# Gates stored where merged blocks go, three ring slots for early expert weights, and edits to the chain and the first turn of a decoder block

## Chip, core and metric

The kernel runs on one core of a Trainium2 chip. The time is device microseconds for one launch, the median of several runs. Four compute engines (TensorE, VectorE, ScalarE, GpSimd) each run their own instruction stream and meet at semaphores; SyncE (SP) issues the transfers.

## What is computed

One decoder layer on 256 tokens of width 1024, all in float32:

```python
h = rms_norm(x, g_mix);  proj = h @ w_in + b_in          # 1024 x 6656
q, k, v, cb, cc, cx, ga, gc = split(proj)
y_attn = sliding_window_attention(rope(q), rope(k), v, sinks) @ w_attn_o
y_conv = (cb * causal_short_conv(cc * cx, w_conv)) @ w_conv_o
merged = sigmoid(ga) * y_attn + sigmoid(gc) * y_conv
x = x + merged @ w_out
h = rms_norm(x, g_ffn)
x = x + moe_ffn(h, ...)   # router takes 4 of 32 experts; per expert
                          # a = g*sigmoid(1.702 g)*(u+1), then a @ w_down
return rms_norm(x, g_final)
```

The 32 experts' weights (up, gate, down, 1024 x 1024 each) are 403 MB, nearly all that the kernel reads.

## The kernel before, in words

**First stage.** The weights of the projections come as 38 pieces of 1 MB (NP1), n = 0 to 37: 26 of w_in (NIN), then w_conv_o and w_attn_o in turn (8), then w_out (4). They land in three small slots in turn. For each piece ScalarE makes a rounded copy wH (L754), and GpSimd (L1319, first half m = 0) and VectorE (L966, m = 1) the remainder wL. TensorE multiplies in three terms: low x wH, high x wH, high x wL (project_T L402, project L415), where high and low are the two parts of the activations. A loop of four turns (L477) does q, conv_C, conv_x, conv_B and the two gates with the attention of a group of heads between them. Then the branch projections (L527) are gated and merged by VectorE (L1091 to L1097), split into mH and mL, and the output projection (L560) adds to x1. In it TensorE also turns x1 (turn_x1) and multiplies it with the router (route).

**Ring.** Eight slots of 2 MB hold expert weights; an expert has six pieces (two of up, gate, down each), and load_expert (L352) issues them on SP's queue in order. In the first stage the same memory holds other things: an "area" is half a slot. Areas 0 to 2 are the three slots for pieces, hH/hL lie in 3, 4, zH/zL in 5, 6, aH/aL in 7, 8, the gates ga and gc in 9, 10, the keys kz in 11, wH and wL in 12 to 15. The first turn of loads waits accordingly (L366 to L373): for areas under 12 for the last branch block and merged_ready, for the rest for the last projection. PHYS gives the order in which slots are used. mH lies in tile mt, mL in tile normed.

**Between the stages.** VectorE scales x1 (scale_x1 L1100), ScalarE and GpSimd cut it into three bfloat16 parts for gathering (cut_high, rest_of, cut_mid, low_of), the inverse root mean square comes by GpSimd (L1304), then VectorE picks the top 4 (L1140 to L1164), TensorE ranks the tokens per expert (L574 to L578), VectorE makes the one-hot G, and TensorE gathers the tokens of expert 0.

**Experts.** For each expert (expert, L656) TensorE runs wide into bank 4 (up), gathers for the next expert, wide into bank 5 (gate), scatters the previous expert's result into banks 0 to 3, turns the activation, and runs wide into bank 7 (down). The first expert does turn_wgt and spread_down_bias instead of a scatter: x1 and the weighted down bias are put into banks 0 to 3 (L651, L653). weights_used frees ring slots. Four experts are straight code, then a loop of seven turns of four. The bias rows that wide adds come to their place by twelve small transfers on SP's queue (L349), on which ScalarE waits before it splits piece 36.

## Time and profile before

| | |
|---|---|
| median of 3 runs | 1216.02 us (1215.77 to 1217.55) |
| profiled execution | 1215.88 us, its span 1214.0 us |
| TensorE busy | 1123.0 us (93%) |
| VectorE, ScalarE, GpSimd busy | 364.9, 236.6, 129.7 us |
| read from HBM | 446.06 MB, 368 GB/s over the span |
| chain that ended last | TensorE 49%, DMA 41%, VectorE 4%, ScalarE 2% |

```profile
GB/s 295 140 166 145 165 154 180 178 391 408 344 429 428 426 427 429 428 427 430 427 429 429 427 430 426 429 430 426 430 426 429 431 426 430 426 429 431 426 429 201
```

This row of the page has the transfers' rate in 40 equal slices of 30 us: eight slices of first stage, then expert weights, with a lower slice at 300 to 330 us. "Idle before" behind a row is the engine's idle time ahead of it and what ended it. The granted clock is TensorE's, as a share of 2.4 GHz.

### The profile page before, as it was taken

The numbers are of one execution on the slowest core, as the hardware profiler recorded it, in microseconds if no ns is written. First come the engines' busy times: TensorE is split into PE (matmuls) and PEld (weight loads), VectorE is DVE, ScalarE is ACT, GpSimd is POOL, SyncE is SP. The second block draws the span as 40 slices with busy tenths as digits, with TensorE's granted clock in tenths as the row PEclk, the third lists the DMA queues.
The fourth block names the chain that finished last, engine by engine and source line by source line (L and its number), as shares of the span: only waits on it lengthen the run. The fifth ranks groups of instructions, "written<-read, shape, count | busy, mean of one in ns | idle before, by whom it ended". The sixth has DMA issues, their size and how long they took to land.

```text
span 1214.0 us, 18031 instructions
## 1 busy us (share of the span) xinstructions
PE 1123.0 (93%) x7446; PEld 574.7 (47%) x7446; DVE 364.9 (30%) x687; ACT 236.6 (19%) x410; POOL 129.7 (11%) x98
## 2 busy tenths in 40 slices
PE   8999999888999999999999999999999998999996
PEld 6899999883333333433333333333333333333332
DVE  5867785663121111111211211111111111111112
ACT  5566654351000100100010001000100110011001
POOL 4453444430000000000000000000000000000000
PEclk9999999998999999999999999999999999999999
DMA  9444445599899999999999999999999999999994
GB/s 295 140 166 145 165 154 180 178 391 408 344 429 428 426 427 429 428 427 430 427 429 429 427 430 426 429 430 426 430 426 429 431 426 430 426 429 431 426 429 201
DMA packets 71250, 447.93 MB, mean 369 GB/s; under 512 B 5433, under 2 KB 45717, under 8 KB 46645
## 3 DMA queue, kind: packets, MB, share of 16 engines
q1 hardware_dynamic: 70752, 446.75, 89.1%
q10 hardware_dynamic: 469, 0.77, 0.2%
q8 instruction: 21, 0.34, 0.1%
q14 instruction: 8, 0.07, 0.0%
HBM read 446.06 MB, written 1.05 MB: 368 GB/s over the span
## 4 chain that ended last, share of the span: by engine, by line
PE 49%; DMA 41%; DVE 4%; ACT 2%; issue 2%; POOL 1%; SPq 0%; POOLq 0%; DVEq 0%; ACTq 0%
PE psum L610 27%; DMA ring<-in_w_gate 20%; DMA ring<-in_w_up 20%; PE psum L411 14%; PE psum L423 2%; PE psum L586 2%; POOL wL L1319 1%; PE psum L634 1%; DVE work L1202 1%; DVE work L1207 1%; DVE work L1204 1%; ACT work L898 1%; DMA ring<-in_w_in 1%; PE psum L601 1%; PE psum L594 1%
## 5 line engine op out<-in xcount | busy, mean ns | idle before, releaser
L610 PE MATMUL psum<-ring,work 128*64 128x512 f32 x3072 | 688.4, 596 | 48.7 <-DMA ring<-in_w_up 25.5
L610 PEld LDWEIGHTS psum<-ring,work 128*64 128x64 f32 x3072 | 211.8, 137 | 473.6 <-issue 369.9
L1200 DVE TENSOR_SCALAR work<-psum 128x512 f32<-128x512 f32 x32 | 22.1, 692 | 422.5 <-PE psum L610 422.5
L1319 POOL TENSOR_TENSOR wL<-ring,wH 128x1024 fp32r<-128x1024 f32 x38 | 103.0, 2720 | 111.5 <-ACT wH L754 111.5
L411 PE MATMUL psum<-hL,wH 128*128 128x256 f32 x384 | 110.5, 288 | 3.5 <-POOL wL L1319 2.9
L411 PE MATMUL psum<-hH,wH 128*128 128x256 f32 x384 | 109.2, 284 | 0.0
L411 PE MATMUL psum<-hH,wL 128*128 128x256 f32 x384 | 109.1, 284 | 0.0
L1202 DVE TENSOR_SCALAR work<-psum 128x512 f32<-128x512 f32 x32 | 22.1, 692 | 284.5 <-PE psum L610 284.5
L1357 POOL COPY chosen<-pick 96x64 bf16 (+1 forms) x32 | 7.5, 234 | 886.9 <-PE psum L634 886.9
L966 DVE TENSOR_TENSOR wL<-ring,wH 128x1024 fp32r<-128x1024 f32 x38 | 77.2, 2034 | 38.5 <-ACT wH L754 38.5
L754 ACT CAST wH<-ring 128x1024 fp32r<-128x1024 f32 x76 | 76.3, 1048 | 29.0 <-PE psum L411 18.1
L411 PEld LDWEIGHTS psum<-hL,wH 128*128 128x128 f32 x384 | 74.2, 193 | 6.4 <-issue 3.3
L411 PEld LDWEIGHTS psum<-hH,wH 128*128 128x128 f32 x384 | 74.3, 194 | 0.0
L411 PEld LDWEIGHTS psum<-hH,wL 128*128 128x128 f32 x384 | 74.2, 193 | 0.0
L907 ACT ACTIVATE work<-work 128x512 f32<-128x512 f32 x32 | 20.2, 630 | 249.6 <-DVE work L1202 249.6
L864 ACT COPY work<-psum 128x64 f32<-128x64 f32 x33 | 7.0, 213 | 301.7 <-PE psum L594 301.7
L621 PE MATMUL psum<-work 64*128 64x512 f32 x256 | 63.6, 615 | 0.7 <-ACT work L903 0.7
L903 ACT COPY work<-psum 128x512 f32<-128x512 f32 x32 | 18.8, 587 | 230.5 <-PE psum L610 230.5
L586 PEld LDWEIGHTS psum<-G,h2b 128*128 128x128 bf16 x1584 | 49.2, 99 | 27.1 <-issue 27.1
L586 PE MATMUL psum<-G,h2b 128*128 128x64 bf16 x1584 | 53.1, 195 | 1.1 <-DVE G L1171 1.1
L621 PEld LDWEIGHTS psum<-work 64*128 64x128 f32 x256 | 22.0, 186 | 41.8 <-issue 40.2
L634 PEld LDWEIGHTS psum<-cst,work 128*128 128x128 f32 x128 | 17.8, 209 | 40.4 <-DVE work L1207 39.7
(199 smaller groups left out, 917.2 us busy)
## 6 DMA issues: line engine op xcount, KB each, us to landing
ring<-in_w_up SPq DMA_DIRECT2D x64, 2048.0 KB, 32.7
ring<-in_w_gate SPq DMA_DIRECT2D x64, 2048.0 KB, 35.4
ring<-in_w_down SPq DMA_DIRECT2D x64, 2048.0 KB, 34.6
ring<-in_w_in SPq DMA_DIRECT2D x26, 1024.0 KB, 4.9
ring<-in_w_conv_o SPq DMA_DIRECT2D x4, 1024.0 KB, 5.2
ring<-in_w_attn_o SPq DMA_DIRECT2D x4, 1024.0 KB, 5.2
ring<-in_w_out SPq DMA_DIRECT2D x4, 1024.0 KB, 5.6
xres<-in_x SPq DMA_DIRECT2D x2, 512.0 KB, 4.2
```

The costliest lines, as they stand in the source:

```text
L411: mm = pe.matmul(bank(b, m * T, T), w[:, par, m, k, :], x[:, k, :], start=(k == 0 and x is low), stop=(k == KB - 1 and w is wL))
L423: mm = pe.matmul(bank(b[t], t * PW, PW).rearrange("p (m n) -> p m n", m=2), x[:, k, t * P:(t + 1) * P], w[:, par, :, k, :], start=(k == 0 ...
L586: mm = pe.matmul(bank(6, k * CW, CW), h2b[:, part, t, k * P:(k + 1) * P], G[:, t, :], start=(t == 0 and part == 0), stop=(t == TT - 1 and ...
L610: mm = pe.matmul(psum[64 * h:64 * h + 64, b, :], src[:, k, :], w[:, k2, h * 512:(h + 1) * 512], start=(bias_of is None and k == 0), stop=( ...
L621: pe.matmul(bank(2 * t + h), S[64 * h:64 * h + 64, t * P:(t + 1) * P], ysb[64 * h:64 * h + 64, :], start=False, stop=False, skip_group_che ...
L634: tr = pe.transpose(bank(5, b * P, P), act_runs[:, b // RUN, :, b % RUN], ident)
L754: nc.scalar.copy(wH[:, par, m, :, :], slot(s).rearrange("p (k n) -> p k n", k=KB)[:, :, m * P:(m + 1) * P],).then_inc(wH_ready, 1)
L907: nc.scalar.activation(sg, gm, ACT.Sigmoid, scale=ALPHA).then_inc(sig_ready, 1)
L966: v.tensor_tensor(wL[:, p2, 1, :, :], slot(s).rearrange("p (k n) -> p k n", k=KB)[:, :, P:2 * P], wH[:, p2, 1, :, :].bitcast(F32), ALU.sub ...
L1200: v.tensor_scalar(uc, psum[:, 4, :], LIMIT, -LIMIT, ALU.min, ALU.max)
L1202: v.tensor_scalar(gm, psum[:, 5, :], LIMIT, None, ALU.min).then_inc(gmin_ready, 1)
L1319: g.tensor_tensor(wL[:, par, 0, :, :], slot(s).rearrange("p (k n) -> p k n", k=KB)[:, :, 0:P], wH[:, par, 0, :, :].bitcast(F32), ALU.subtr ...
```

## The change

Gates go to mt and normed, where merged blocks are written afterwards; hH to aL move up one area, the keys down to area 3. Ring slots 5, 2 and 3 come first, with pieces 0 and 1 issued among the loads of the first stage, and the waits of the first turn are by area. The projections take the terms with wH first and wait for wL behind them. One wait on merged_ready goes. Between the stages: five matmuls before the ranks, the spread inside the first gather, turn_wgt ahead of the first expert, two VectorE steps less, the last scale_x1 behind the mean square. spread_down_bias moves to expert 29, and the last group of four experts is straight code too.

```diff
@@ line 54
-PHYS = [2, 3, 4, 5, 1, 0, 6, 7]
+PHYS = [5, 2, 3, 4, 1, 0, 6, 7]
+EARLY = 2
...
@@ line 82
     c[:, C_M1:C_M1 + 2 * P] = np.where((dist >= 0) & (dist < P), 0.0, MASKED)
-    c[:, C_IOTA:C_IOTA + CW] = np.where(np.arange(CW) < CAP, np.arange(CW), -5 * T)
+    c[:, C_IOTA:C_IOTA + CW] = np.where(np.arange(CW) < CAP, np.arange(CW) - NEVER, -5 * T - NEVER)
...
@@ line 135
         mt_at = -(-nc.sbuf_base // 32) * 32
-        sb("mt", [P, KB, T])
+        mt = sb("mt", [P, KB, T])
...
@@ line 168
             return ring_at + s * KB * PW * 4
-        hH, hL = parts("hH", at_slot(3), [P, KB, T]), parts("hL", at_slot(4), [P, KB, T])
-        zH, zL = parts("zH", at_slot(5), [P, KB, T]), parts("zL", at_slot(6), [P, KB, T])
-        aH, aL = parts("aH", at_slot(7), [P, KB, T]), parts("aL", at_slot(8), [P, KB, T])
+        hH, hL = parts("hH", at_slot(4), [P, KB, T]), parts("hL", at_slot(5), [P, KB, T])
+        zH, zL = parts("zH", at_slot(6), [P, KB, T]), parts("zL", at_slot(7), [P, KB, T])
+        aH, aL = parts("aH", at_slot(8), [P, KB, T]), parts("aL", at_slot(9), [P, KB, T])
...
         mH, mL = parts("mH", mt_at, [P, KB, T]), parts("mL", normed_at, [P, KB, T])
-        ga = slot(9).rearrange("p (k t) -> p k t", k=KB)
-        gc = slot(10).rearrange("p (k t) -> p k t", k=KB)
-        kz = slot(11).rearrange("p (g h t) -> p g h t", g=NKV, h=2)
+        ga = mt
+        gc = normed.rearrange("p t (k c) -> p (t k) c", c=T)
+        kz = slot(3).rearrange("p (g h t) -> p g h t", g=NKV, h=2)
...
@@ line 319
+            def load_run(e, c, r):
+                s = phys((c * EP + r) % RING)
+                src = experts[r // RUNS][bass.ds(e, 1), :, r % RUNS, :, :]
+                sp.dma_start(ring[:, s, :], src.rearrange("a p r n -> p (a r n)")).then_inc(slot_full[s], 16)
+            load_run(0, 0, 0)
...
@@ line 342
                 n += 1
+                if n == NIN + 5:
+                    sp.wait_ge(blocks_done, 2 * NIN)
+                    load_run(0, 0, 1)
...
@@ line 351
                 for r in range(EP):
-                    s = phys((c * EP + r) % RING)
-                    wait(r, s)
-                    src = experts[r // RUNS][bass.ds(e, 1), :, r % RUNS, :, :]
-                    sp.dma_start(ring[:, s, :], src.rearrange("a p r n -> p (a r n)")).then_inc(slot_full[s], 16)
+                    if wait(r, phys((c * EP + r) % RING)):
+                        load_run(e, c, r)
...
                         p = c * EP + r
+                        if first and p < EARLY:
+                            return False
...
                                     slot_split(max(n for n in range(NP1) if n % RING1 == area) + RING1)
-                                elif area < 12:
+                                elif area < 8:
+                                    sp.wait_ge(blocks_done, 2 * (NIN + 2 * NKV - 1))
+                                elif area < 10:
                                     sp.wait_ge(blocks_done, 2 * (NIN + 2 * NKV))
-                                    sp.wait_ge(merged_ready, NKV)
...
                                     sp.wait_ge(blocks_done, 2 * NP1)
+                        return True
...
@@ line 385
                     e = sp.value_load(eid[0:1, bass.ds(j, 1)], min_val=0, max_val=NE - 1)
-                    load_expert(e, 0, lambda r, s: None)
+                    load_expert(e, 0, lambda r, s: True)
...
@@ line 405
                         between()
+                    pe.wait_ge(wH_ready, n * 2 + (m + 1))
+                    for k in range(KB):
+                        for x in (low, high):
+                            pe.matmul(bank(b, m * T, T), wH[:, par, m, k, :], x[:, k, :], start=(k == 0 and x is low),
+                                      stop=False)
...
                     for k in range(KB):
-                        for w, x in ((wH, low), (wH, high), (wL, high)):
-                            mm = pe.matmul(bank(b, m * T, T), w[:, par, m, k, :], x[:, k, :],
-                                           start=(k == 0 and x is low), stop=(k == KB - 1 and w is wL))
+                        mm = pe.matmul(bank(b, m * T, T), wL[:, par, m, k, :], high[:, k, :], start=False, stop=(k == KB - 1))
...
                 high, low = src
-                pe.wait_ge(wL0_ready, n + 1)
-                pe.wait_ge(wL1_ready, n + 1)
+                pe.wait_ge(wH_ready, n * 2 + 2)
                 def block(t, ks):
-                    for k in ks:
-                        for x, w in ((low, wH), (high, wH), (high, wL)):
+                    for k, x, w in [(k, x, wH) for k in ks for x in (low, high)] + [(k, high, wL) for k in ks]:
+                        if True:
+                            if w is wL and k == ks[0] and t == 0:
+                                pe.wait_ge(wL0_ready, n + 1)
+                                pe.wait_ge(wL1_ready, n + 1)
...
@@ line 555
-            pe.wait_ge(merged_ready, NKV)
...
@@ line 569
+            for n in range(WARM):
+                pe.matmul(bank(2), ident, cst[:, 0:512], start=True, stop=True)
...
@@ line 577
-            def gather(nth):
+            def gather(nth, between=None):
...
                 for k in range(KB):
+                    if k == KB // 2 and between is not None:
+                        between()
...
@@ line 612
-            def scatter(nth, chunk):
+            def scatter(nth, chunk, fresh=False):
...
                         pe.matmul(bank(2 * t + h), S[64 * h:64 * h + 64, t * P:(t + 1) * P],
-                                  ysb[64 * h:64 * h + 64, :], start=False, stop=False, skip_group_check=True,
+                                  ysb[64 * h:64 * h + 64, :], start=fresh, stop=False, skip_group_check=True,
...
@@ line 639
                 for t in range(TT):
-                    tr = pe.transpose(bank(6, t * P, P)[0:NE], wgt[:, t, 0:NE], ident)
+                    tr = pe.transpose(bank(3, t * P, P)[0:NE], wgt[:, t, 0:NE], ident)
...
@@ line 648
                     for h in range(2):
-                        pe.matmul(bank(2 * t + h), ident, xres[:, t, h * 512:(h + 1) * 512], start=True, stop=False,
+                        pe.matmul(bank(2 * t + h), ident, xres[:, t, h * 512:(h + 1) * 512], start=False, stop=False,
...
+            def at(j, n):
+                return isinstance(j, int) and j == n
...
                 pe.wait_ge(picked, j + 1)
-                if j is not first_expert:
+                if not at(j, 0):
                     pe.wait_ge(S_ready, j)
-                if j is first_expert:
-                    turn_wgt()
                 wide(4, xe, c, 0, uses, 0)
-                if j is first_expert:
+                if at(j, 0):
...
                 wide(5, xe, c, RUNS, uses, 1)
-                if j is first_expert:
+                if not at(j, 0):
+                    scatter(j, j, fresh=at(j, 1))
+                if at(j, NE - UNROLL + 1):
                     spread_down_bias()
-                else:
-                    scatter(j, j)
...
             pe.wait_ge(low_ready, NKV)
-            gather(0)
-            spread_r(0, 5)
+            gather(0, lambda: spread_r(0, 5))
+            turn_wgt()
             pe.wait_ge(bias_out, 16 * 12)
-            first_expert = 0
-            for c in range(UNROLL):
-                expert(c, c, lambda p: 16 * (p // RING + 1))
-            first_expert = None
-            with pe.Fori(1, NE // UNROLL) as it:
+            def group(it):
...
                     expert(it * UNROLL + c, c, uses)
+            group(0)
+            with pe.Fori(1, NE // UNROLL - 1) as it:
+                group(it)
+            group(NE // UNROLL - 1)
...
@@ line 908
             act_e.wait_ge(wT_turned, 1)
-            nc.scalar.copy(wT[:, :], psum[0:NE, 6, 0:256]).then_inc(wT_ready, 1)
+            nc.scalar.copy(wT[:, :], psum[0:NE, 3, 0:256]).then_inc(wT_ready, 1)
...
@@ line 971
             v.memset(u[:, :, 0:2], 0.0)
-            v.memset(pos[:, :, NE:NE + 1], NEVER)
+            v.memset(pos[:, :, NE:NE + 1], 0.0)
...
@@ line 1097
+            sums = small[:, 12:20].rearrange("p (t i) -> p t i", t=TT)
...
@@ line 1124
                 n += 1
-                scale_x1(i)
+                if i < NKV - 1:
+                    scale_x1(i)
...
                     rest_of(i)
+                if i == NKV - 2:
+                    dve.wait_ge(ssq_ready, 2 + 2 * (NKV - 1))
+                    steps.link(v.tensor_reduce(small[:, 6:8], sums[:, :, 0:NKV - 1], AX.X, ALU.add))
+                    steps.link(v.tensor_scalar(small[:, 6:8], small[:, 6:8], 1.0 / D, EPS, ALU.mult, ALU.add))
...
             dve.wait_ge(ssq_ready, 2 + 2 * NKV)
-            steps.link(v.tensor_reduce(small[:, 6:8], small[:, 12:20].rearrange("p (t i) -> p t i", t=TT), AX.X, ALU.add))
-            ms(6)
+            v.scalar_tensor_tensor(small[:, 8:10], sums[:, :, NKV - 1:NKV].rearrange("p t i -> p (t i)"), 1.0 / D, small[:, 6:8],
+                                   ALU.mult, ALU.add).then_inc(ms_ready, 1)
+            scale_x1(NKV - 1)
...
@@ line 1149
             steps.link(ins)
-            steps.link(v.tensor_copy(topf, topi[:, :, :]))
...
                 ins = v.tensor_tensor(onehot[:, t], count_up[:, 0:NE].unsqueeze(1).broadcast_to([P, TOPK, NE]),
-                                      topf[:, t, 0:TOPK].unsqueeze(2).broadcast_to([P, TOPK, NE]), ALU.is_equal)
+                                      topi[:, t, 0:TOPK].unsqueeze(2).broadcast_to([P, TOPK, NE]), ALU.is_equal)
...
@@ line 1161
                                               -NEVER, Mf[:, :, :], ALU.add, ALU.mult))
-            steps.link(v.tensor_scalar(pos[:, :, 0:NE], pos[:, :, 0:NE], NEVER, None, ALU.add))
...
@@ line 1212
+                dve.wait_ge(gathered, nth + 1)
...
                     dve.wait_ge(weights_used, used)
...
```

## Rows read from the trace of the kernel before

**Rows 1.** Chain that ended last, in order of time: start us, us, what

```profile
298.62 1.06 PE psum L651 x2
...
306.00 1.05 PE psum L653 x2
...
315.71 6.87 PE psum L610 x32
...
342.87 6.87 PE psum L610 x32
...
620.89 3.68 PE psum L610 x16
...
709.00 3.68 PE psum L610 x16
...
1153.25 35.41 DMA ring<-in_w_gate
```

**Rows 2.** Windows: us, five engines' busy time, TensorE's clock, DMA share, GB/s

```profile
306.00:314.00 8.00, 7.54 (x34) 2.87 (x36) 2.31 (x8) 0.59 (x1) 0.23 (x1) 1.00 0.34 115
360.00:1180.00 820.00, 759.92 (x4714) 286.72 (x4714) 149.02 (x375) 75.91 (x129) 6.79 (x29) 1.00 1.01 428
```

**Rows 3.** SP's queue in order of time: start us, us, line, what

```profile
235.05 8.85 SPq L349 DMA_DIRECT2D bias<-bcut  x12
...
267.06 0.80 SPq L357 DMA_DIRECT2D ring<-in_w_up  x2
286.05 3.76 SPq L357 DMA_DIRECT2D ring<-in_w_gate  x2
...
312.10 0.33 SPq L357 DMA_DIRECT2D ring<-in_w_up  x1
```

**Rows 4.** First turn, in order of time on SP, ScalarE, VectorE and TensorE

```profile
16.93 0.40 SPq L307 DMA_DIRECT2D ring<-in_w_in  x1
...
31.27 1.99 ACT L754 CAST wH<-ring 128x1024 fp32r<-128x1024 f32 x2
...
35.85 3.78 DVE L953 COPY work<-work 32x512 f32<-32x512 f32 x4
...
34.79 10.17 PE psum L411 x72
```

**Rows 5.** Branch and output projections: waits, timeline, one window, bias transfers' landings

```profile
PE psum L411 <- POOL wL L1319: 1.1, 3, 0.4
...
239.15 0.58 PE L423 MATMUL psum<-wH,mL 128*128 128x256 f32 x1 [2.88 <-DVE mL L1096]
...
240.00:242.00 2.00, 2.00 (x11) 2.00 (x11) 1.64 (x1) 0.26 (x1) 1.78 (x1) 0.50 0.19 45
...
246.76 2.00 ACT L754 CAST wH<-ring 128x1024 fp32r<-128x1024 f32 x2 [6.50 <-PE psum L423]
...
L349 SPq DMA_DIRECT2D bias<-bcut x12: 605/606/1530, 235.0 to 243.3; - x12
...
DMA to landing us min/median/max: 1.9/2.9/5.1
```

**Rows 6.** From x1 to the first expert: timeline and a window; opening matmuls last

```profile
267.02 0.76 DVE L1124 TENSOR_TENSOR xres<-psum,xres 128x256 f32<-128x256 f32 x2 [3.68 <-PE psum L423]
...
271.24 0.41 DVE L1141 SCALAR_TENSOR_TENSOR work<-psum,small,brt 128x32 f32<-128x32 f32 x2 [0.92 <-PE psum L553]
...
275.67 2.72 PE L586 MATMUL psum<-G,h2b 128*128 128x64 bf16 x48 [1.09 <-DVE G L1171]
...
281.31 8.13 PE L610 MATMUL psum<-ring,work 128*64 128x512 f32 x32
...
289.37 1.57 PE L586 MATMUL psum<-G,h2b 128*128 128x64 bf16 x48
...
274.00:283.00 9.00, 6.58 (x65) 4.51 (x67) 5.95 (x27) 1.86 (x3) 0.00 (x0) 0.50 1.03 404
...
2.62 6.73 PE L466 MATMUL psum<-ring 128*128 128x512 f32 x10 [2.62 <-POOL ring L1309]
```

## The prediction

> **What bounds the kernel now.** I read the chain of waits first, then the load queue, then the windows of the stretch between the two stages. From 620.9 us on the chain alternates between weight landings and short stretches of TensorE. Three experts take 88.11 us (620.89 to 709.00), 29.37 each, or 4.895 per 2 MB piece; TensorE alone needs 27.15 for an expert, seen where its weights are there early (315.71 to 342.87) [rows 1]. So each expert of the late part has 2.22 us of slack on TensorE, and the load stream sets the end. In the bulk the stream moves 428 GB/s and the DMA engines are full. Only between 306 and 314 us do they stand at a 0.34 share, so 5.3 us are empty [rows 2]. The queue's issues say why: piece 8 goes out at 286.05, when the first expert's first slot is free, but piece 12 only at 312.10 [rows 3]. The ring of eight was full, and TensorE was busy with the down bias, 8 pairs from 298.62 to 307.05 [rows 1]. From piece 12's issue to the landing of piece 189, the last on which the chain waits (1153.25 + 35.41, so 1188.67 [rows 1]), it is 876.6 us for 178 pieces; 25.3 us follow to the end of the span. Thus three things can shorten the kernel: an earlier first slot release (now 286.05), no hole after it, and less behind the last landing.
>
> **Slots for expert weights.** Piece 0 goes out behind the small loads, before the fourth w_in piece; piece 1 behind the fifth branch piece. With the gates in mt and normed, three slots are no longer tied to merged_ready. In the loop over the first stage the DMA engines are about half idle, so I cost the transfers at nothing. The cover: the fourth w_in piece is issued at 16.93 and not split by ScalarE before 31.27 [rows 4]; 4.9 us of queue ahead of it leave more than 4 us. If that cover were gone, piece 0 would cost up to 4.9 us. What do early slots bring? The third one brings little: its load still stands in SP's program behind the last branch loads and the twelve bias moves, which hold SP for 8.85 us from 235.05 [rows 3]. With two pieces there, six remain. Four start at about 240.5 (the end of the bias moves, 243.9, less 3.5 us won before it, below) and are in by 260.2; pieces 6 and 7 wait for wH and wL, free after the last projection (267.06 now, some 260.5 after), and are in by about 270.5. Without the early pieces the fill would end at about 280. I get the first release at 277.8 below. So the early slots are worth 1 to 2 us; the ring is full again, and the release decides.
>
> The Trainium skill ("DMA: Bandwidth & Descriptors", Queues, rings and completion order) says that an issuing engine's transfers are consumed in ring order on each DMA engine. That speaks against loading early: pieces 3 to 5 stand behind piece 0. By that rule alone the first stage could lose the 4.9 us; the rows on ScalarE's first use give it room. This rule is the third rival.
>
> **Bias spread from the first expert to the 30th.** The eight pairs take 8.43 us wherever they stand [rows 1]. In the first expert they made the hole. Without them TensorE frees slots 0, 3.4 (16 matmuls of wide, half of the 6.87 [rows 1]), 9.1, 12.6, 20.1 and 23.5 us after the first release, against 4.895 us a piece: 0.5 us of hole stays. From piece 8's issue to piece 189's landing I expect 876.6 + 4 x 4.895 + 0.5 = 896.7 us. With the present 286.05 that is 1182.7 instead of 1188.67: 6.0 us gained. But at expert 29 (counted from 0) the 8.43 us lie on TensorE ahead of wide(7), and only two experts with 2.22 us of slack each follow. 8.43 - 4.44 = 4.0 us come back at the end. The ring covers the loads meanwhile (8.4 us is under two pieces of eight). Bounds: 0 if the last landing still decides, 8.4 if nothing is absorbed. The unrolled last group I cost at nothing: the present first group is straight code as well and its cadence is the loop's; bounds 0 to 1 us. No less, because it does no less work.
>
> **High half first, and the dropped wait.** In the branch projections TensorE waits three times for wL, 1.1 us in all [rows 5]; wH is there 2.4 us before wL, so the 16 matmuls with wH cover it: -1.1. In the first turn TensorE waits 2.9 us for wL before block 3, until 34.79 [rows 4], and runs some 3 us of it at half clock. With the high half it can start at 32.3. Behind that comes q's rotation on VectorE, whose copies start at 35.85 [rows 4] and which ends near 41.7, so scores cannot follow block 4 much earlier, and then the softmax chain. I take -2.4, bounds 0 and -3.6.
>
> The first output projection no longer waits for all merged blocks. It starts at 239.15, 2.88 us after its predecessor, and its first matmuls run at the lower clock, 0.50 in 240 to 242 [rows 5]. The fourth merged block is needed only after 36 matmuls, 4.3 us: covered. That frees 2.9 us of waiting and 1.7 of slow clock, 4.6. But ScalarE stands behind it: it splits piece 36 only at 246.76 and, by its program, not before all bias moves have landed. The last is issued at 243.3 and they take 1.9 to 5.1 us [rows 5], so it is there at 245.2 or later. With 3.5 us from before it is 241.7. Then follow the split (1.9), two square sums (1.2), cut_high (.6) and turn_piece (.6): route(0) can start at 246.1, where it starts at 252.67 now, though TensorE would be there at 244.6. So of 4.6 us only 3.1 arrive. Sum for the end of the last projection: 2.4 + 1.1 + 3.1 = 6.6 us earlier (bounds 1 and 9).
>
> **The chain from x1 to the first expert.** Now 286.05 - 267.02 = 19.0 us lie between x1 and the first release. All of it runs at half clock from 270 on [rows 6]. VectorE: scale_x1(3) now follows the rstd input and ScalarE's cut, rest_of(3) ends at +4.85 instead of +3.3, and the logits, now at +4.22, start 0.65 later. Dropping the copy to topf gives back 0.21, dropping the addition of NEVER 0.23. TensorE: 5 warming matmuls, ten instructions, start at +3.9. In the opening the same ten took 6.73 us, five at 0.86 and five at 0.43 [rows 6]. I take the clock to rise after the third: they end at +9.35, later than M_ready at +7.6. So M's matmuls come 2.1 us later than now, and the gather starts at +10.55 instead of +8.65: 1.9 us lost. In return it runs at full clock: 48 matmuls and the spread take 2.05 (1.57 and 0.64 at 289.37, less overlap) against 3.64 now (275.67 to 279.3); ScalarE's copy of slot_r is hidden by the interleaving (0.27); turn_wgt leaves the path (0.68); the first 16 of wide take 3.44 against 4.53 (of the 8.13 that all 32 take [rows 6]). 1.9 - 1.6 - 0.3 - 0.7 - 1.1 = -1.7. Bounds: -4.5 (clock never low), +4.4 (low for all ten and through the expert's start).
>
> The Trainium skill ("TensorE: Matmul & The Clock Gate", What's actually happening) says that the slow clock is the default and activity releases it. By that the warming pays; the rows agree that the clock was 0.50 while TensorE waited and ran small matmuls. No row here shows what ten large ones do at this place.
>
> **Sum**, against the profiled 1214.0 us of span and 1215.88 of time (the median of the runs is 1216.02, the same within 0.01%): first release 286.05 - 6.6 - 1.7 = 277.75; + 896.7 = 1174.45; + 25.3 = 1199.8; + 4.0 = 1203.8; + 1.9 outside the span = 1205.7.
>
> **Rivals.** (1) Forecast as above, 0.50, its own range 1202 to 1209. (2) More arrives: the bias moves land in time, block 3 gains 3.6 and the warming ends before M_ready: 1.5 + 1.2 + 2.3 less, 1200.7; 0.14. For it: every lost us above is a place where two engines finish within 2 us. (3) The first stage gains nothing, because weights ahead of w_in pieces eat it, or VectorE's chain gives it back: + 6.6, 1212.3; 0.13. Against it: ScalarE waits for a landing only once. (4) The warming runs slow throughout and ends at +12.5: + 6.1, 1211.8; 0.15. (5) The change doesn't act as it says, the slots being filled anyway: only the title's part falls, 1 to 2 us, 1207.2; it lies within (1). (6) Slower: the stream itself. Landings now go to slots in another order. The 896.7 us hang on 428 GB/s; each per cent is 9.0 us, and from 1.4% (below 422) the kernel is slower than before; at 2% it is 1223.6. Against it: the DRAM reads are the same. 0.04; with mixtures of (3), (4) and a bias spread not absorbed (+4.4) it makes 0.06 slower in all.
>
> **Numbers.** 0.2% is 2.4 us, about what can be told from no change. Faster 0.88, within 0.2% 0.06 ((3) and (4) together, or either with an unabsorbed spread), slower 0.06. The range takes in (2) to (4): 1199 to 1213; some 2 in 10 lie outside.
>
> **What would show it.** The first ring release near 278; no empty stretch of DMA at 300 to 310 but one ahead of the first release, some 6 us; the last landing on which the chain waits near 1174; the last wide starting about 4 us after its weights are in; matmuls at 239 without a wait; a wait at route(0); the M matmuls 2 us later against x1. It is wrong if the stream doesn't follow the first release, or if the bias spread costs its full 8.4 us late.

## The result, and the profile of the changed kernel

The changed kernel takes 1206.97 us (median of 5 runs, 1206.07 to 1210.74) where the kernel before, run beside it, takes 1216.3 (1215.77 to 1217.92): a ratio of 0.9925, 95% interval 0.9909 to 0.9942. The prediction was 1205.7 within 1199 to 1213. The profiled run took 1206.97, with a span of 1205.2.

Below, columns and views are those of the section of rows; "release" is the issue of piece 8, the first load that waits for a slot used by the first expert. SP's queue of the changed kernel:

```profile
188.92 0.37 SPq L308 DMA_DIRECT2D ring<-in_w_attn_o  x1
...
235.00 8.51 SPq L360 DMA_DIRECT2D bias<-bcut  x12
243.61 1.01 SPq L326 DMA_DIRECT2D ring<-in_w_gate  x2
...
263.15 0.80 SPq L326 DMA_DIRECT2D ring<-in_w_up  x2
278.94 3.76 SPq L326 DMA_DIRECT2D ring<-in_w_gate  x2
...
300.71 3.76 SPq L326 DMA_DIRECT2D ring<-in_w_up  x2
```

The last output projection ends (263.15, pieces 6 and 7 go out) 3.9 us earlier than before, the release is 7.1 us earlier, and piece 12, which stood behind the bias spread, 11.4 us earlier [rows 3]. But the bias moves still begin at 235.00, as before: up to there the changed first stage has won nothing. The load of attn_o at 188.92, issued behind the loop over the heads, is even 1.3 us later (187.63 before).

The timeline of ScalarE and TensorE from the output projections to the first expert's end. L571 is route, the product of one of the four parts of x1 with the router (route(0) the first, route(3) the last); Mb is M, the table of chosen experts, from which TensorE makes the ranks:

```profile
244.82 2.00 ACT L777 CAST wH<-ring 128x1024 fp32r<-128x1024 f32 x2 [5.04 <-DMA bias<-bcut]
...
248.66 1.08 PE L571 MATMUL psum<-wr,work 128*128 128x32 f32 x8 [0.95 <-ACT work L895]
...
265.44 1.08 PE L571 MATMUL psum<-wr,work 128*128 128x32 f32 x8 [0.79 <-DVE work L1163]
266.35 4.54 PE L590 MATMUL psum<-cst 128*128 128x512 f32 x10
271.05 0.19 PE L593 MATMUL psum<-Mb,tri 128*128 128x32 bf16 x1 [0.16 <-DVE Mb L1190]
...
272.20 0.86 PE L607 MATMUL psum<-G,h2b 128*128 128x64 bf16 x24 [0.86 <-DVE G L1200]
...
293.90 0.75 PE L655 MATMUL psum<-cst,work 128*128 128x128 f32 x4 [2.37 <-DVE work L1236]
```

ScalarE waits 5.04 us for the bias moves, and through it TensorE at route(0). The five warming matmuls of the code are ten instructions in the trace, called the ten warming matmuls below. They take 0.45 us each, so the clock never fell here, and they end 0.16 us before M is ready. In the first expert there is a new wait of 2.37 us: TensorE is ready to turn the activation before VectorE has made it, since the bias spread no longer stands between. Windows of the stretches after it:

```profile
276.00:280.00 4.00, 4.00 (x21) 1.51 (x18) 1.38 (x6) 0.34 (x1) 0.00 (x0) 1.00 0.40 137
...
296.00:298.00 2.00, 2.00 (x6) 0.49 (x4) 1.21 (x6) 0.00 (x0) 0.00 (x0) 0.50 1.03 442
300.00:304.00 4.00, 4.00 (x22) 1.33 (x20) 0.00 (x0) 0.00 (x0) 0.00 (x0) 1.00 0.67 213
...
360.00:1180.00 820.00, 764.08 (x4756) 289.10 (x4754) 146.22 (x365) 74.61 (x127) 6.55 (x28) 1.00 1.01 428
```

The DMA engines stand empty for 4 x 0.60 = 2.4 us ahead of the release and 4 x 0.33 = 1.3 us around the issue of piece 12, where 5.3 us were empty before [rows 2]. Behind the new wait TensorE ran at 1.2 GHz (0.50 granted) from 296.0 to 299.4. In the bulk the stream moves 428 GB/s, as before. The end of the chain of waits:

```profile
1082.84 35.85 DMA ring<-in_w_gate
...
1124.31 1.05 PE psum L672 x2
...
1131.68 1.05 PE psum L674 x2
...
1188.41 7.11 PE psum L631 x32
```

The last landing on which the chain waits is 1118.69, at expert 29. Then come the eight bias pairs (1124.31 to 1132.73), and from there to the last wide the chain is compute alone: the weights are always there first. Before, it still waited for the landing at 1188.67 [rows 1]. One part of the difference between the two spans is not the change: from the issue of the output's store to the end of the span it is 5.4 us in the profile before (1208.58 to 1214.0) and 4.4 us here (1200.83 to 1205.2), and 4.3 to 4.4 in all other profiles but one.

### The profile page after: what moved, and what is told of

Its sections match the earlier page's. It is cut to its first block, busy times and chain, and to the rows that moved or that the text cites. A ratio compares the mean times of both kernels' runs of the same rounds, so it can differ in the third digit from the quotient of the medians.

```text
span 1205.2 us, 18121 instructions
## 1 busy us (share of the span) xinstructions
PE 1122.0 (93%) x7456; PEld 573.6 (48%) x7456; DVE 367.8 (31%) x686; ACT 236.5 (20%) x410; POOL 130.1 (11%) x98
## 4 chain that ended last, share of the span: by engine, by line
PE 50%; DMA 38%; DVE 6%; ACT 2%; issue 2%; SPq 1%; DVEq 0%; ACTq 0%
PE psum L631 30%; DMA ring<-in_w_gate 20%; DMA ring<-in_w_up 17%; PE psum L424 8%; PE psum L428 4%; PE psum L607 2%; PE psum L655 1%; DVE work L1231 1%; DVE work L1236 1%; DVE work L1233 1%; PE psum L441 1%; ACT work L921 1%; DVE wL L989 1%; ACT wH L777 1%; DMA ring<-in_w_in 1%
## 5 line engine op out<-in xcount | busy, mean ns | idle before, releaser
L424 PE MATMUL psum<-hL,wH 128*128 128x256 f32 x384 | 95.3, 286 | 1.7 <-ACT wH L777 1.1
L424 PE MATMUL psum<-hH,wH 128*128 128x256 f32 x384 | 94.1, 283 | 0.0
L989 DVE TENSOR_TENSOR wL<-ring,wH 128x1024 fp32r<-128x1024 f32 x38 | 80.8, 2131 | 40.4 <-ACT wH L777 40.4
L428 PE MATMUL psum<-hH,wL 128*128 128x256 f32 x384 | 53.9, 283 | 0.3 <-POOL wL L1349 0.3
L428 PEld LDWEIGHTS psum<-hH,wL 128*128 128x128 f32 x384 | 49.5, 192 | 0.5 <-POOL wL L1349 0.5
L655 PE MATMUL psum<-cst,work 128*128 128x128 f32 x128 | 23.9, 309 | 16.0 <-DVE work L1236 16.0
## 6 DMA issues: line engine op xcount, KB each, us to landing
ring<-in_w_up SPq DMA_DIRECT2D x64, 2048.0 KB, 32.7
```

The source lines that it names most:

```text
L424: pe.matmul(bank(b, m * T, T), wH[:, par, m, k, :], x[:, k, :], start=(k == 0 and x is low), stop=False)
L428: mm = pe.matmul(bank(b, m * T, T), wL[:, par, m, k, :], high[:, k, :], start=False, stop=(k == KB - 1))
L655: tr = pe.transpose(bank(5, b * P, P), act_runs[:, b // RUN, :, b % RUN], ident)
L989: v.tensor_tensor(wL[:, p2, 1, :, :], slot(s).rearrange("p (k n) -> p k n", k=KB)[:, :, P:2 * P], wH[:, p2, 1, :, :].bitcast(F32), ALU.sub ...
```

## Experiments

The kernel before was timed again beside each group; its medians were 1216.7 (beside no_warming, old_order, no_early_slots, merged_wait), 1216.5 (bias_first, only_bias_moved, bias_at_28, bias_at_24) and 1216.0 (the last four of the table). The intervals of the ratios are about ±0.0015, 2 us, and so a single difference of one or two microseconds between two medians is not settled by them. The changed kernel was not timed beside the others; against it, a difference of medians and one of ratios can come apart: no_early_slots is 3.5 us longer by medians and 1.7 by ratios, merged_wait 3.3 and 2.3, no_collision 2.9 and 1.8 shorter. Of the kernels made from the changed one, only quarter_first and all_three have an interval that doesn't overlap with its own. What carries the other verdicts are the stations of the profiled run: the attn_o load (end of the loop over heads), the issue of pieces 6 and 7 (end of the last projection), the release, piece 12, and the span. Each kernel has one profile, and it need not be a typical run: no_collision's is the shortest of its five, those of only_bias_moved, no_early_slots and quarter_first are the longest of theirs.

| kernel | median us | ratio to before | attn_o | last proj. | release | piece 12 | span |
|---|---|---|---|---|---|---|---|
| before | 1216.3 | | 187.63 | 267.06 | 286.05 | 312.10 | 1214.0 |
| changed | 1206.97 | 0.9925 | 188.92 | 263.15 | 278.94 | 300.71 | 1205.2 |
| no_warming | 1208.99 | 0.9931 | 189.09 | 263.49 | 280.74 | 302.09 | 1207.6 |
| bias_first | 1207.77 | 0.9930 | 189.04 | 263.27 | 279.04 | 305.10 | 1206.2 |
| old_order | 1208.38 | 0.9930 | 188.74 | 264.81 | 280.59 | 302.09 | 1206.6 |
| no_early_slots | 1210.49 | 0.9939 | 188.85 | 263.90 | 279.65 | 301.43 | 1210.2 |
| merged_wait | 1210.24 | 0.9944 | 188.13 | 264.32 | 281.45 | 303.22 | 1209.3 |
| only_bias_moved | 1214.71 | 0.9978 | 188.63 | 266.63 | 287.17 | 308.76 | 1214.5 |
| bias_at_28 | 1204.76 | 0.9905 | 189.02 | 263.42 | 279.20 | 300.95 | 1203.3 |
| bias_at_24 | 1205.83 | 0.9917 | 186.20 | 260.56 | 276.33 | 297.77 | 1202.1 |
| no_collision | 1204.04 | 0.9910 | 186.17 | 260.61 | 276.38 | 296.45 | 1200.8 |
| bias_wait_later | 1206.44 | 0.9922 | 188.03 | 261.04 | 278.17 | 299.94 | 1204.6 |
| quarter_first | 1202.72 | 0.9890 | 189.05 | 263.97 | 279.74 | 299.82 | 1203.1 |
| all_three | 1199.63 | 0.9867 | 185.63 | 258.65 | 275.79 | 295.87 | 1196.8 |

**Without the warming matmuls.** The loop of WARM matmuls behind route(3) is left out:

```
-            for n in range(WARM):
-                pe.matmul(bank(2), ident, cst[:, 0:512], start=True, stop=True)
```

> The kernel after without the five warming matmuls ahead of the ranks. Theory (activity there keeps the clock up): the clock is 0.5 from some 270 us to the first expert as before the change, the gather's 48 matmuls take 2.7 instead of 1.6 us, the first slot release comes some 2.9 us later (near 282 instead of 278.9) and the time is 2 to 3 us above the kernel after (1209 to 1210). Rival (the clock was up there by chance, the warming itself only delays): release and time the same or up to 0.5 us less.

TensorE now waits for M, and its clock is low from 268.9 to 275.7:

```profile
271.36 0.21 PE L591 MATMUL psum<-Mb,tri 128*128 128x32 bf16 x1 [4.51 <-DVE Mb L1188]
```

From last projection to release it is 17.25 us for 15.79. The warming is worth 1.5 us here, about half of the 2.9 expected, and it delays nothing. The time agrees in its direction (2.0 us by medians, 0.7 by ratios) and settles nothing by itself.

**Bias spread back in the first expert.** All else is as changed:

```
-                if not at(j, 0):
-                    scatter(j, j, fresh=at(j, 1))
-                if at(j, NE - UNROLL + 1):
-                    spread_down_bias()
+                if at(j, 0):
+                    spread_down_bias()
+                else:
+                    scatter(j, j)
```

(Its first matmul of each pair also starts the bank afresh again, as before the change.)

> The kernel after with the down bias spread in the first expert again, all else as after. Theory: TensorE now waits 2.4 us for VectorE in the first expert and falls to the lower clock there; the 8.4 us fill that wait, so piece 12 is released some 4.5 us later than after (305.2 for 300.7) and the DMA is empty for as long; at the end 3.5 us of lag go. Sum about 1 us above the kernel after (1208). Rival (the prediction's sum holds): 2.0 us above. Rival (the late bias costs its whole 8.4 us): 4 us below.

Piece 12 goes out 4.4 us later, the wait of 2.37 us and the fall of the clock are gone, and the chain ends on landings again. The span is 1.0 us longer. So in this pair of profiles the move to expert 29 by itself, with all else in place, gains 1 us: 4.4 at the start, 3.5 given back at the end. The medians, 0.8 us apart, agree and don't settle it.

**The old order of the projections.** project_T and project take wH and wL of each k together, and wait for both first:

```
-                    pe.wait_ge(wH_ready, n * 2 + (m + 1))
-                    for k in range(KB):
-                        for x in (low, high):
...
                     pe.wait_ge((wL0_ready, wL1_ready)[m], n + 1)
                     for k in range(KB):
...
+                        for w, x in ((wH, low), (wH, high), (wL, high)):
...
```

> The kernel after with the terms of each projection in the old order and the wait for wL ahead of them. Theory (with the high half first the first turn collides VectorE with GpSimd: scores come later, although TensorE is earlier; in the branch projections it saves the waits): the second turn of the loop begins 1 to 1.5 us earlier than after, the branch projections get back 1.1 to 1.3 us of waits, the time stays within 1 us of after (1206 to 1208). Rival (the early weights made the first turn late, the order helps everywhere): the first turn stays late or gets later, and the time is 1.3 to 4 us above after.

The loop over heads ends at the same time as in the changed kernel, within 0.2 us. The new order gains 1.3 us in the branch stage (bias moves at 236.16 for 235.00) and 0.5 in the projections, but in the first turn nothing. That part of the theory fell, and with 1208.38 so did its time (1206 to 1208). Yet the collision it spoke of is gone in this run: VectorE's add of the first turn took 0.69 us, 2.77 in the changed kernel. What hid it is that block 3 starts at 35.84 for 32.90, and that the opening came 0.5 us later. What VectorE has in it, no_collision tests.

**No early slots.** Pieces 0 and 1 are loaded with the others, when the gates, the branches and the bias moves are through:

```
-EARLY = 2
+EARLY = 0
-            load_run(0, 0, 0)
...
-                if n == NIN + 5:
-                    sp.wait_ge(blocks_done, 2 * NIN)
-                    load_run(0, 0, 1)
...
+                                if p < 2:
+                                    sp.wait_ge(blocks_done, 2 * NIN)
```

> The kernel after with no expert piece ahead of the bias moves: pieces 0 and 1 are issued where the others are, same slots. Theory (the ring is full at the first release anyway, the release decides): the fill ends near 284 instead of before 278, piece 8 starts some 4 us later, but the wait for piece 12's slot at 300 takes most of that back: 1 to 2 us above the kernel after (1208 to 1209). Rival (early pieces shorten the stream by their own length): 2 x 4.9 = 9.8 us above it (1216.8).

Its windows:

```profile
276.00:280.00 4.00, 4.00 (x22) 1.63 (x20) 1.94 (x10) 1.06 (x1) 0.00 (x0) 1.00 1.02 422
300.00:304.00 4.00, 4.00 (x22) 1.37 (x20) 0.00 (x0) 0.00 (x0) 0.00 (x0) 1.00 0.99 422
```

The stream has no hole at all; it is bound from its start at 244.37. The landing ahead of the bias pairs comes at 1123.79 for 1118.69, 5.1 us later, and the median is 3.5 us longer (1.7 by ratios). The attn_o load stands at 188.85: the two early transfers cost the first stage nothing, so the third rival's mechanism (weights ahead of w_in pieces in the rings) shows no cost here.

**The merged wait restored.** `pe.wait_ge(merged_ready, NKV)` in place of `NKV - 1`:

> The kernel after with TensorE waiting for all four merged blocks before the first output projection. Theory: a wait of 3.0 us at 235.6 and low clock behind it; route(0), now at 248.66 behind the bias moves, starts near 252.4; release and time 3 to 4 us later (1210 to 1211). Rival (the bias moves hide it): within 1.3 us of after.

TensorE waits 2.88 us for mL again. Its loop ended 0.8 us early in this run, and still the last projection is 1.2 us late: 2.0 us of the wait reach it. Another 1.3 come from the clock, which fell at 267.2 and made the warming matmuls 5.88 us long. Together 3.3, as much as the medians differ (2.3 by ratios); that the two figures meet is partly chance, since the release of this profile is only 2.5 us later, for its early loop.

**Only the bias spread moved.** The kernel before, with the spread at expert 29 and the unrolled last group that it needs:

> The kernel before with one edit: the bias spread goes from the first expert to expert 29, last group as straight code. Theory: the hole of 5.3 us between 306 and 314 shrinks below 1 us, 3.5 to 4.0 us come back at the end: 1 to 1.5 us below the kernel before. Rival (nothing is absorbed at the end): 3 us above it.

The ratio is 0.9978 (0.9966 to 0.9991), 1 to 4 us gained, with piece 12 at 308.76 for 312.10. Its profile, the longest of seven runs, shows no gain in the span (1214.5 for 1214.0): the first wide took 9.65 us in it, 8.13 before [rows 6], and so the release is 1.1 us later, not the same. The ratio fits the 1 us of bias_first.

**Bias spread at expert 28.** `if at(j, NE - UNROLL)` in place of `NE - UNROLL + 1`:

> The kernel after with the bias spread one expert earlier, at 28. Theory (each expert that follows absorbs 2.2 us): 2.2 us below the kernel after (1204.8), with the last gate landing waited for by 1 to 2 us less lag. Rival (the place does not matter): the same time as after.

With the same stations up to piece 12 the last wide begins at 1186.52 for 1188.41 and the span is 1.9 us shorter: one expert more, with 2.22 us of slack, absorbs so much.

**Bias spread at expert 24**, with two unrolled groups at the end:

> The kernel after with the bias spread at expert 24 and two groups as straight code at the end. Theory: seven experts absorb all of it, the chain ends on the last landings again: 3.5 us below the kernel after (1203.5). Rival (straight code costs TensorE instruction loads): above 1205.

The chain ends on landings, so all the lag is absorbed. But the median, 1205.83, is not the expected 1203.5, and it lies above the 1205 that was to speak for the rival. It is 1.1 us above bias_at_28's, which the intervals don't settle, and its runs spread over 6 us. In its profile two stretches behind the spread are longer than elsewhere: the last wait is for a landing at 1176.00, 878.2 us behind piece 12, where it is 876.8 in bias_first (1181.90), and the store of the output ends 6.2 us behind its issue, not 4.4. Whether either has to do with the second straight group, no run shows; the rival stays open.

Its release was 2.6 us earlier, and that had nothing to do with the bias: its loop over heads ended at 186.20. Up to there it is the code of the changed kernel, but GpSimd's subtraction in the first turn began behind VectorE's add:

```profile
41.20 0.69 DVE L983 TENSOR_TENSOR ph<-ph,work 128x512 f32<-128x512 f32 x1
42.02 6.61 POOL L1350 TENSOR_TENSOR wL<-ring,wH 128x1024 fp32r<-128x1024 f32 x2 [3.33 <-ACT wH L778]
```

The add took 0.69 us where it took 2.77 in the changed kernel. GpSimd was late because TensorE's clock was at 1.2 GHz from 32.7 to 36.1 in this run, in block 3, on which ScalarE's copy follows. So the same code can win or lose this race from run to run: of the nine profiles with this code up to there, the add took 2.76 to 2.78 us in eight and 0.69 in this one. The next experiment makes of this a test.

**No collision in the first turn.** GpSimd begins its part of the fourth piece of a turn only when VectorE has finished the query's rotation:

```
                 for c in range(1, 7):
+                    if c == 3:
+                        pool.wait_ge(rotated, i + 2)
                     split_low(i * 6 + (2 + c), (2 + c) % RING1, c % 2)
```

> The changed kernel with one wait more: GpSimd begins the low half of the stage's fourth weight piece of a turn (n = 5, 11, ...) only when VectorE has signalled the rotated query. Theory (the collision in the first turn): in the changed kernel GpSimd's subtraction began at 41.47 us, VectorE's add of the same turn (41.61) took 2.77 us in place of 0.69, softmax began 48.94, and the loop ended 1.3 us later than before (attn_o load issued 188.92 against 187.63). With the wait the add takes 0.7 us, GpSimd starts about 0.8 us later (42.3) and its two subtractions end where VectorE's end, the softmax begins near 46.9, the attn_o load is issued at 186.5 to 187.0 and the first release of the ring comes at about 276.7; time 2.0 us under the changed kernel, about 1205. Rival (the add is long by the way the profile records it, or softmax then waits for another engine): the add is short but the attn_o load stays at 188.7 to 189.1, and the time stays at 1207. Later turns are the same in both, since GpSimd begins there after the add anyway (84.92).

First the kernel before, VectorE's add and GpSimd's subtraction in order of start:

```profile
40.99 0.69 DVE L959 TENSOR_TENSOR ph<-ph,work 128x512 f32<-128x512 f32 x1
...
44.09 5.73 POOL L1319 TENSOR_TENSOR wL<-ring,wH 128x1024 fp32r<-128x1024 f32 x2 [5.60 <-ACT wH L754]
```

Then the changed kernel, with TensorE's wait for the add and the start of softmax:

```profile
41.47 2.37 POOL L1349 TENSOR_TENSOR wL<-ring,wH 128x1024 fp32r<-128x1024 f32 x1 [2.37 <-ACT wH L777]
...
41.61 2.77 DVE L982 TENSOR_TENSOR ph<-ph,work 128x512 f32<-128x512 f32 x1
...
44.51 0.71 PE L505 MATMUL psum<-ring,ph 64*128 64x128 f32 x8 [2.16 <-DVE ph L982]
...
48.94 0.74 DVE L1044 SCALAR_TENSOR_TENSOR work<-psum,cst 128x256 f32<-128x256 f32 x2
```

And no_collision:

```profile
41.04 0.69 DVE L982 TENSOR_TENSOR ph<-ph,work 128x512 f32<-128x512 f32 x1
...
41.91 6.57 POOL L1349 TENSOR_TENSOR wL<-ring,wH 128x1024 fp32r<-128x1024 f32 x2 [3.38 <-ACT wH L777]
...
46.12 0.74 DVE L1044 SCALAR_TENSOR_TENSOR work<-psum,cst 128x256 f32<-128x256 f32 x2
```

In the changed kernel the earlier third block freed ScalarE 2.6 us earlier, and with it GpSimd's subtraction, which now began 0.14 us ahead of VectorE's add. The add then took 2.77 us and ended 0.54 us behind GpSimd's end (43.84). With the wait it takes 0.69, softmax starts 2.8 us earlier, the loop ends 2.75 us earlier and so does, within 0.2 us, all up to the release; the median is 2.9 us under the changed kernel's (1.8 by ratios). Of the 2.8 us the collision has some 2.1; 0.6 come from the opening, where TensorE's clock stayed high in this run (both VectorE's chain and block 3 start 0.57 us earlier). In the first expert the clock didn't fall either, behind the same wait of 2.37 us: piece 12 follows the release after 20.1 us, not 21.8. The edit has no part in that, and so the span of this profile, 4.4 us shorter, shows more than the edit brings.

**ScalarE's wait for the bias moves put later**, behind its split of piece 36 and the squares, ahead of cut_high(0):

```
-            act_e.wait_ge(bias_out, 16 * 12)
             for i in range(NKV):
...
+                if i == 0:
+                    act_e.wait_ge(bias_out, 16 * 12)
                 cut_high(i)
```

> The changed kernel with ScalarE's wait for the twelve bias moves put behind its half of the split of piece 36 and the squares, ahead of its cut of the bias's high part. Theory (in the changed kernel ScalarE is held 5.04 us by the bias moves, at 244.82, and through it the first routing product at 248.66): the split and the squares come before the moves land, the first routing product comes near 247.6, the last projection ends near 262.1 (263.15), the first release near 277.9 (278.94), the time 1.0 us lower, about 1206. Rival (VectorE's chain of the same stage or TensorE's own projections are late next): route(0) moves by under 0.3 us and the time by nothing. Were the bias moves no hold at all, ScalarE's waiting would only change its name.

```profile
246.65 0.97 PE L571 MATMUL psum<-wr,work 128*128 128x32 f32 x8
...
263.32 1.47 PE L571 MATMUL psum<-wr,work 128*128 128x32 f32 x8 [0.78 <-DVE work L1164]
264.60 5.85 PE L590 MATMUL psum<-cst 128*128 128x512 f32 x10
270.29 0.18 PE L593 MATMUL psum<-Mb,tri 128*128 128x32 bf16 x1
```

Route(0) comes 2.0 us earlier, 0.9 of them from the first turn of this run, 1.1 from the edit, and without a wait; the last projection ends 2.1 us earlier. So the bias moves did hold that stretch. Yet the release is only 0.8 earlier: the clock fell at 263.9, the ten warming matmuls took 5.85 us and ended behind M. So in this profile the edit's gain was lost to the clock; the ratio, 0.9922, can't be told from 0.9925.

**A quarter of the spread in the first expert, three quarters at expert 28:**

```
-                if at(j, NE - UNROLL + 1):
-                    spread_down_bias()
+                if at(j, 0):
+                    spread_down_bias((0,), fresh=True)
+                if at(j, NE - UNROLL):
+                    spread_down_bias((1, 2, 3))
```

> The changed kernel with the bias spread cut in two: one of its four quarters (two matmuls, about 2.1 us) in the first expert, where the changed kernel's TensorE waits 2.37 us for VectorE (293.90), three at expert 28. Theory (that wait and the fall of the clock after it, 296.2 to 299.6 at 1.2 GHz, are the price of moving the whole spread away; a quarter fills the wait for nothing): no wait over 0.5 us on VectorE in the first expert, the clock stays at 2.4 GHz from there, the fifth piece of the ring (piece 12) is issued near 299.0 (300.71), and the late spread is behind the landings by nothing or little, since it is shorter by a quarter (6.3 for 8.4 us) and stands an expert earlier; the chain of waits ends on landings. Time 3.5 to 5 us under the changed kernel: 1202 to 1203.5. Rival (the stream sets the end alone, and what the first expert lost was already made up by the seven early pieces): only the gain of the spread at expert 28, 1204.8, with piece 12 earlier and nothing from it.

```profile
294.70 0.75 PE L656 MATMUL psum<-cst,work 128*128 128x128 f32 x4 [0.27 <-DVE work L1241]
```

The chain of waits of the same kernel:

```profile
1143.85 34.97 DMA ring<-in_w_gate
...
1186.31 7.11 PE psum L631 x32
```

The wait is 0.27 us, the clock stays at 2.4 GHz, piece 12 follows the release after 20.1 us, and the last wait is for a landing (1178.82). The median is 4.2 us under the changed kernel's (4.3 by ratios) and 2.0 under bias_at_28. Against the latter the profile doesn't show it: the span is 1203.1 for 1203.3, for the last landing comes 879.0 us behind piece 12, 2.2 more than in bias_first; this profile is the longest of its four runs, and why its stream was slower is open.

**All three edits together:**

> The changed kernel with all three edits: GpSimd's wait in the turn, ScalarE's wait for the bias moves later, the bias spread in a quarter and three. If each does what its own theory says and they lie one behind the other ahead of the stream: 2.0 + 1.0 + 4.0 us under the changed kernel, 1200. First release near 275.7, piece 12 near 296, chain ending on landings. Rival (the stream is already bound from its start at 243.6, so that an earlier first release brings less than its full size once no hole is left): 1202 to 1203.

```profile
1138.89 33.66 DMA ring<-in_w_gate
...
1180.04 7.11 PE psum L631 x32
```

1199.63 us (1197.53 to 1200.83), ratio 0.9867 (0.9849 to 0.9884): 7.3 us under the changed kernel. The gains add up within the noise, 2.9 + 0.5 + 4.2 = 7.6 (by ratios 1.8 + 0.4 + 4.3 = 6.5, for 7.0). Its clock, too, fell behind route(3) (17.1 us from the last projection to the release). Some 1.3 us more would be there at the high clock, but no kernel with ScalarE's wait put later kept it. Its last waited landing is 1172.55, and 1172.55 - 275.79 = 896.8 us after the release.

## Why the prediction held, and where it did not

The median is 1.3 us above the forecast. By its own steps, against the profiled span of 1205.2:

| term | predicted | measured |
|---|---|---|
| first turn | -2.4 | +1.3 |
| branch stage | -1.1 | -1.3 |
| dropped wait, to the last projection | -3.1 | -3.9 |
| chain to the release | -1.7 | -3.2 |
| release | 277.75 | 278.94 |
| release to last landing | 896.7 | 898.5 |
| behind it, lag of the bias included | 29.3 | 27.8 |
| span | 1203.8 | 1205.2 |

For the last landing's row I take the landing at 1118.69 and twelve pieces of 4.895 us more, 1177.4, since the chain no longer shows it.

**First turn: the step that failed.** Block 3 could start at 32.3, said the prediction; it started at 32.90, and at 32.32 in no_collision. But "then the softmax chain" was sized as if VectorE's rotation would take its old time. It had it only while GpSimd was idle, and what moved GpSimd into it was the gain itself. Without the collision the loop ends 1.5 us earlier than before (186.17 for 187.63), not 2.4; the copies of VectorE's rotation start where they did (35.87 for 35.85), and from them to the softmax it is 10.25 us, 11.62 before, 12.50 in the changed kernel. So the collision turned a gain of 1.4 us into a loss of 0.9, and the opening, at the low clock for 3.4 us in this profile, added 0.6. That last part is the run's, not the change's. Rival (3) named the place, "VectorE's chain gives it back", but priced it at the whole 6.6.

The Trainium skill ("SBUF — State Buffer", SBUF: two separate sides) says that VectorE with two SBUF inputs and a GpSimd operation that reads SBUF take the shared port pair as an exclusive lock, whichever starts first. The trace agrees: GpSimd started 0.14 us ahead, and the add ends 0.54 us behind GpSimd's end; in bias_at_24, with the add ahead, it took 0.69 us.

**Branch stage** was right, and old_order shows the same 1.3.

**Dropped wait.** The mechanism was right: route(0) waits for ScalarE and ScalarE for the bias moves, and bias_wait_later gains 1.1 there. The gain at route(0) is 252.67 - 248.66 = 4.0 us. I had counted 3.1: the moves were in at 244.8 where I took 245.2, and from there to route(0) it is 3.8 us, not 4.4.

**The chain.** I counted the low clock for the first six of ten warming matmuls; it never fell in this run. The two cases show in the table above: from the last projection to the release it is 15.8 us in eight of the kernels that warm, 17.1 in the three whose clock fell (merged_wait, bias_wait_later, all_three), 17.25 without warming, 19.0 before. So the warming goes with 1.5 us less where the clock stays up, and with 0.1 where the clock falls just before it. My 17.3 was the slow case. Rival (4), low for all ten, appeared in none. M's matmuls come 0.6 us later against x1 than before (7.87 for 7.24 us), not 2 us.

**The hole.** The slot of piece 12 was to come 20.1 us after the release. It did so in no_collision and quarter_first, but in the changed kernel after 21.8. I had seen that the spread was in the way of the slots, not that it covered VectorE's activation. The wait of 2.37 us by itself is within my sum, which took the loop's own cadence; the 1.7 us are the clock that fell behind it. They are most of the 1.8 by which the term from the release to the last landing is too small. This was no accident of one run: of the ten kernels whose first expert has the wait of 2.37 us, the clock fell behind it in nine, all but no_collision.

**Early slots: mis-sized, by the profiles.** I gave them 1 to 2 us, since the fill without them would end near 280, from a start at 240.5. The start was 244.37, as the first turn gave nothing: eight pieces of 4.895 us from there end at 283.5, 4.6 behind the changed kernel's release. So much would be lost without the early pieces, and no_early_slots shows 5.1 in the chain, 3.5 in the medians and 1.7 in the ratios. So rival (5) may have cost more than its 1 to 2 us. For the same reason the DMA engines stood empty for 2.4 us ahead of the release and not for the 6 that I had named.

**Lag of the late bias.** 4.0 predicted. The landing worked out above is 1177.4; in bias_first and all_three the end lies 24.3 us behind the last landing, so 1205.2 - 1177.4 - 24.3 = 3.5. The other 1.0 of the 1.5 us in the table's row is no gain of the change: it is the store of the output, which ended 1.0 us later in the profile of before, and with it my 25.3. At expert 28 the lag shrinks by about the slack of one expert, as the rows had it.

Errors thus cancelled, and that the sum came within 1.4 us of the span is in part luck: to the last projection 2.7 us less came than predicted, the chain and the end gave 1.5 more each, and 1.8 went to the clock in the first expert.

Left open: what decides whether the clock falls behind route(3). In the changed kernel and in bias_wait_later TensorE waits 0.8 us there, and it fell in the second alone. One thing goes with it in all eleven profiles with warming: the eight whose clock stayed up had a wait of 0.95 to 1.8 us that ended between 244 and 250, seven of them at route(0), and the three whose clock fell had none there. No run varies that alone, but two of the three have ScalarE's wait put later, and removing the wait at route(0) was the aim of that edit; so its gain and the loss behind route(3) may belong together. In the opening, too, the clock fell near 13 us in some profiled runs (the changed kernel's, quarter_first's) and not in others. Within one kernel's runs the times spread by 1 to 7 us; that these places make the spread is only argued, since each kernel has a single profile.

## What to carry to other kernels

When a wait is shortened, list what starts earlier with it, on every engine, and what it will then run beside: here 2.6 us won on TensorE brought GpSimd's subtraction in front of a VectorE operation on the critical path. Work that stands in the way of the slots may also fill another engine's latency; leave as much of it as fills that for nothing (a quarter, here) and move the rest to where enough slack follows. A race between two engines decided by a tenth of a microsecond can go either way from run to run; fix the order by a wait. And a gain ahead of a stretch of tight timing can be taken back by TensorE's clock, so read the granted clock at each station before adding terms up.

## What the runs showed of the hardware

A VectorE addition of 128x512 with both inputs in SBUF takes 0.69 us alone and 2.77 us when GpSimd has begun a subtraction of 128x1024 just before it; the other way round, GpSimd's two subtractions took 6.57 us with VectorE ahead (41.91) and 2.37 and 2.36 each where they went first. These figures fit one engine waiting for the other, not the two sharing at half rate, and order decides who waits.

Two transfers of 2 MB put among the 1 MB pieces of the first stage delayed nothing that could be seen (188.85 without them, 188.92 with).

The same wait of 2.37 us in the first expert was followed by a stretch at 1.2 GHz in nine of ten kernels (296.0 to 299.4 in the changed one) and by none in no_collision. With a wait of 0.27 us in its place (quarter_first, all_three) the clock stayed at 2.4 GHz in both.
